# Four transposes per head instead of six, with the small probability blocks side by side

## The reference

```
# fox: forgetting attention
s = einsum(q, k) * scale + c[t] - c[s];  p = softmax(where(kpos <= qpos, s, NEG));  o = p @ v
# swa: window of 128, 2 kv heads, partial rotary, a sink per head in the denominator,
#      meta tokens (the first 16 keys) always visible
m = max(s_band.max, s_meta.max, sink);  denom = sum(p_band) + sum(p_meta) + exp(sink - m)
# mla: q and kv from low-rank latents, one rotary key shared by all heads
qf = [q_nope, rope(q_rope)];  kf = [k_nope, rope(k_rope)];  o = softmax(causal(qf @ kf)) @ v
# each: h = layer_norm(alpha * h + o @ w_o);  h = layer_norm(alpha * h + conv_glu_ffn(h))
```

## Time and profile before

| | |
|---|---|
| time, median of 3 runs | 1342.8 us (1342.38 to 1342.91) |
| profiled execution | 1340.74 us, of which span 1338.9 |
| PE busy | 1300.1 us, 97% of the span |
| DVE, ACT, POOL busy | 936.4, 816.1, 232.7 us |
| DMA | 202.81 MB, mean 151 GB/s |
| chain that ended last | PE 84%, DVE 7%, ACT 5%, issue 2% |
| in it | L381, L385, L384 23% each; L531 2%, L549 2% |

### The profile page before, as it was taken

The page is one execution under the profiler, slowest core; times in us unless marked ns, Lnnn a source line. Parts: engine busy times, 40 slices in busy tenths (PEclk is TensorE's granted clock), DMA queues, the critical chain, the costliest instruction groups (busy, mean ns, idle before and its releaser), DMA issues.

```text
span 1338.9 us, 30076 instructions
## 1 busy us (share of the span) xinstructions
PE 1300.1 (97%) x10437; PEld 1256.8 (94%) x10437; DVE 936.4 (70%) x1869; ACT 816.1 (61%) x1649; POOL 232.7 (17%) x216
## 2 busy tenths in 40 slices
PE   7999999999998999999998999999999999999997
PEld 7899999999987999999987899999999999999996
DVE  4865777765687877765678687776567666777764
ACT  5565766654565676664576677665456656766644
POOL 1000044420000034430001003433000000244300
PEclk9999999999999999999999999999999999999999
DMA  6432455556421455556442145555644333455572
GB/s 261 144 110 81 141 185 182 181 184 192 130 93 49 129 176 186 183 166 204 151 127 79 33 142 178 187 170 184 193 140 148 109 123 127 139 187 185 180 222 78
DMA packets 56724, 202.81 MB, mean 151 GB/s; under 512 B 6208, under 2 KB 8256, under 8 KB 56512
## 3 DMA queue, kind: packets, MB, share of 16 engines
q1 hardware_dynamic: 56640, 201.68, 46.8%
HBM read 200.61 MB, written 1.05 MB: 151 GB/s over the span
## 4 chain that ended last, share of the span: by engine, by line
PE 84%; DVE 7%; ACT 5%; issue 2%; DMA 1%; DVEq 0%; ACTq 0%; SPq 0%
PE ps L381 23%; PE ps L385 23%; PE ps L384 23%; PE ps L531 2%; PE ps L549 2%; DVE w_lo L1254 2%; PE ps L420 1%; ACT probs L885 1%; PE ps L514 1%; PE ps L426 1%; PE ps L423 1%; ACT w_hi L835 1%; DMA raw<-in_weights 1%; PE ps L495 1%; ACT L937 1%
## 5 line engine op out<-in xcount | busy, mean ns | idle before, releaser
L1254 DVE TENSOR_TENSOR w_lo<-raw,w_hi 128x1024 fp32r<-128x1024 f32 x377 | 460.9, 1224 | 228.5 <-ACT w_hi L835 226.8
L381 PE MATMUL ps<-h_hi,w_hi 128*128 128x272 f32 (+1 forms) x1752 | 509.3, 291 | 2.2 <-DVE q_rope L1511 1.0
L385 PE MATMUL ps<-h_hi,w_lo 128*128 128x272 f32 (+1 forms) x1752 | 503.4, 287 | 0.0
L384 PE MATMUL ps<-h_lo,w_hi 128*128 128x272 f32 (+1 forms) x1752 | 501.8, 286 | 0.0
L835 ACT ACTIVATE w_hi<-raw 128x1024 fp32r<-128x1024 f32 x377 | 395.3, 1050 | 151.0 <-PE ps L381 140.6
L381 PEld LDWEIGHTS ps<-h_hi,w_hi 128*128 128x128 f32 x1752 | 329.0, 188 | 9.0 <-issue 5.4
L384 PEld LDWEIGHTS ps<-h_lo,w_hi 128*128 128x128 f32 x1752 | 329.6, 188 | 0.3
L385 PEld LDWEIGHTS ps<-h_hi,w_lo 128*128 128x128 f32 x1752 | 329.1, 188 | 0.0
L381 PE MATMUL ps<-hid_hi,w_hi 128*128 128x272 f32 (+2 forms) x636 | 184.1, 289 | 0.3 <-ACT y L1087 0.2
L1228 POOL TENSOR_TENSOR gated<-y 128x272 f32<-128x272 f32 x88 | 134.6, 1530 | 276.3 <-DVE y L1666 261.7
L384 PE MATMUL ps<-hid_lo,w_hi 128*128 128x272 f32 (+2 forms) x636 | 182.0, 286 | 0.0
(11 more groups left out here) (187 smaller groups left out, 1757.3 us busy)
## 6 DMA issues: line engine op xcount, KB each, us to landing
raw<-in_weights SPq DMA_DIRECT2D x377, 512.0 KB, 3.7
cst<-in_consts SPq DMA_DIRECT2D x1, 1795.5 KB, 11.7
h<-in_x SPq DMA_DIRECT2D x2, 544.0 KB, 5.6
out<-h SPq DMA_DIRECT2D x8, 128.0 KB, 1.8
```

The source lines that it names most:

```text
L381: m = pe.matmul(b, whi, xhi, start=n == 0, stop=False)
L384: pe.matmul(b, whi, xlo, start=False, stop=False)
L385: m = pe.matmul(b, wlo, xhi, start=False, stop=n == len(tiles) - 1)
L1254: return dve.tensor_tensor(out_, a_, b_, op)
```

## The change

The score columns of a head are ordered anew. Chunk 1 comes first (0 to 143), then chunk 0 (144 to 159), then chunk 2 (160 to 431). The keys are stored with the last 16 tokens in front: `KCOL` says which columns a chunk takes, chunk 2 all of them and the others from column 16 on, so their 16 first keys come directly. In chunk 2 the last 16 keys stand first. `probs` has the same 432 columns per head as `scores`. Columns 128 to 175 of it now hold three blocks of 16 keys side by side: the end of chunk 1, all of chunk 0, and the last 16 keys of chunk 2. One transpose of 128 columns from 128 on turns them all, into partitions 0 to 47 (the rest of its rows is not used). Three more turn the large blocks. So:

- `turn`: four transposes of 128x128 per head.
- `copy_turned`: three copies, 128x384, 32x32 (two groups of 16 columns) and 16x16.
- `mix`: still three matmuls per head, of 272, 128 and 3 x 16 columns; the third is for the three small blocks and writes the first 16 columns of three stretches of 128.
- `v_tok`'s third block now needs on partitions 0 to 47 the values that go with them: a copy of the first 16 rows of its second block, of the first 16 rows of its first, and the last 16 tokens. ACT issues two small SBUF-to-SBUF DMAs per layer (`corner_values`), and the first mix of a layer waits for them.
- Each copy of keys is made in two parts, 16 and 256 columns; the rows of decays get one copy more; the masks' columns are rolled for chunk 2; fewer cells are cleared at the start.

```diff
-SCOL = (0, 16, 160, 432)
-PCOL = (0, P, 3 * P)
-PT1, PT2, PTW = T, T + P + TAIL, T + P + 2 * TAIL
+SCOL = ((P + TAIL, P + 2 * TAIL), (0, P + TAIL), (P + 2 * TAIL, P + 2 * TAIL + T))
+KCOL = ((TAIL, 2 * TAIL), (TAIL, P + 2 * TAIL), (0, T))
+TURNED = (0, P + 3 * TAIL, 2 * P + 3 * TAIL, P)
+PT1, PT2, PTW = T, T + P, T + P + 3 * TAIL
...
-        probs = sb("probs", [P, 4, PW])
+        probs = sb("probs", [P, 4, SW])
...
-                one(PT1 + TAIL - P, 1, P)
-                one(PTW - P, 2, 2 * P, TAIL)
-                one(0, 0, 0)
-                one(N_META, 1, 0)
-                one(N_META + P, 2, 0)
-                one(PT1 + TAIL, 2, P).then_inc(transposed, 1)
+                for n, col in enumerate(TURNED):
+                    t = pe.transpose(b[:, n * P:(n + 1) * P], pr[:, col:col + P], ident)
+                t.then_inc(transposed, 1)
...
+                if m == 0:
+                    pe.wait_ge(v_corners, 32 * (a + 1))
-                        ins = pe.matmul(ps[HD * s:HD * s + HD, 6, lo:T], v_tok[:, t, col:col + HD],
-                                        probs_t[:, s, c0:c0 + T - lo], start=n == 0, stop=n == 2)
+                        o, pt = ps[HD * s:HD * s + HD, 6], probs_t[:, s]
+                        if t < 2:
+                            dst, src = o[:, (0, N_META + P)[t]:T], pt[:, (0, PT1)[t]:(PT1, PT2)[t]]
+                        else:
+                            dst = o[:, 0:3 * P].rearrange("p (g c) -> p g c", g=3)[:, :, 0:TAIL]
+                            src = pt[:, PT2:PTW].rearrange("p (g c) -> p g c", g=3)
+                        ins = pe.matmul(dst, v_tok[:, t, col:col + HD], src, start=t == 0, stop=t == 2)
...
+            def corner_values(cols):
+                for n, chunk in enumerate((1, 0)):
+                    act.dma_start(v_tok[TAIL * n:TAIL * n + TAIL, 2, 0:cols],
+                                  v_tok[0:TAIL, chunk, 0:cols]).then_inc(v_corners, 16)
...
-                act.activation(probs_t[:, s, 0:PT2], ps[:, 4 + s, 0:PT2], ACT.Copy)
-                act.activation(probs_t[0:TAIL, s, PT2:PTW], ps[0:TAIL, 4 + s, PT2:PTW],
+                b = ps[:, 4 + s]
+                act.activation(probs_t[:, s, N_META:PT2], b[:, 0:3 * P], ACT.Copy)
+                act.activation(probs_t[0:32, s, PT2:PT2 + 2 * TAIL].rearrange("p (g c) -> p g c", g=2),
+                               b[0:32, 3 * P:4 * P].rearrange("p (g c) -> p g c", c=TAIL)[:, 0:8:7, :], ACT.Copy)
+                act.activation(probs_t[32:48, s, PT2 + 2 * TAIL:PTW], b[32:48, 4 * P - TAIL:4 * P],
                                ACT.Copy).then_inc(pt_copied, 1)
...
-                        copy(keys[:, m, :], b).then_inc(bank_free, 2)
+                        copy(keys[:, m, 0:TAIL], b[:, 2 * P:T])
+                        copy(keys[:, m, TAIL:T], b[:, 0:2 * P]).then_inc(bank_free, 2)
```

More of the change, by code:

```diff
@@ L228, in c @@
             return cst[0:rows, a:b]
+        rope_parts = scores[0:32].rearrange("p s c -> p (s c)")
         mean_sq, mean = y[:, 2, :], y[:, 3, :]
@@ L513, in score_pair @@
                         r = HD * s
-                        ins = pe.matmul(ps[0:hi_q - lo, 2 + s, SCOL[ch]:SCOL[ch + 1]],
-                                        queries[r:r + HD, m, lo:hi_q], keys[r:r + HD, m if fox else m // 4, 0:hi],
+                        ins = pe.matmul(ps[0:hi_q - lo, 2 + s, slice(*SCOL[ch])], queries[r:r + HD, m, lo:hi_q],
+                                        keys[r:r + HD, m if fox else m // 4, slice(*KCOL[ch])],
                                         start=not fox, stop=not fox or ch == 2)
@@ L544, in mix @@
                 pe.wait_ge(o_split, PAIRS * a + m)
-                for n, (t, lo, c0) in enumerate(((0, 0, 0), (1, P, PT1), (2, 2 * P, PT2))):
+                if m == 0:
+                    pe.wait_ge(v_corners, 32 * (a + 1))
+                for t in range(3):
                     for s in range(2):
@@ L1095, in copy_vt @@
                             act.wait_ge(lat_scale, 1)
-                        act.activation(v_tok[0:rows, chunk, half * 512:half * 512 + 512], ps[0:rows, 2 + n % 2],
+                        r0 = 32 if chunk == 2 else 0
+                        act.activation(v_tok[r0:r0 + rows, chunk, half * 512:half * 512 + 512], ps[0:rows, 2 + n % 2],
                                        ACT.Copy, scale=lat_col[0:rows, 1, chunk:chunk + 1]).then_inc(vt_copied, 1)
@@ L1527, in rope_keys @@
                             for r in range(2):
-                                ins = copy(keys[64 * r:64 * r + 64, g, :], q_rope[64 * g:64 * g + 64, 0, :])
+                                src = q_rope[64 * g:64 * g + 64, 0, :]
+                                copy(keys[64 * r:64 * r + 64, g, 0:TAIL], src[:, 2 * P:T])
+                                ins = copy(keys[64 * r:64 * r + 64, g, TAIL:T], src[:, 0:2 * P])
                         ins.then_inc(roped, 1)
@@ L1587, in rope_key_rows @@
                         dve.wait_ge(bank_free, LAYERS[a]["a"][2] + 6)
-                        own.link(tt(scores[0:32, 0, 0:T], gated[0:32, :], cos[0:32], ALU.mult))
+                        one, two, both = (rope_parts[:, n * T:n * T + T] for n in range(3))
+                        own.link(tt(one, gated[0:32, :], cos[0:32], ALU.mult))
                         dve.wait_ge(swapped, base)
-                        tt(scores[0:32, 1, 0:T], ps[0:32, 7, 0:T], sin[0:32], ALU.mult).then_inc(roped, 1)
+                        tt(two, ps[0:32, 7, 0:T], sin[0:32], ALU.mult).then_inc(roped, 1)
                         dve.wait_ge(roped, base)
-                        tt(scores[0:32, 0, 0:T], scores[0:32, 0, 0:T], scores[0:32, 1, 0:T],
-                           ALU.add).then_inc(key_roped, 1)
+                        tt(both[:, 0:TAIL], one[:, 2 * P:T], two[:, 2 * P:T], ALU.add)
+                        tt(both[:, TAIL:T], one[:, 0:2 * P], two[:, 0:2 * P], ALU.add).then_inc(key_roped, 1)
                     def rope_r(m):
@@ L1611, in take_k @@
                         b = bank(p, 2)
-                        tt(keys[0:64, 2 * m, :], b[0:64], kv_rstd[0:64], ALU.mult)
-                        tt(keys[0:64, 2 * m + 1, :], b[64:128], kv_rstd[64:128], ALU.mult).then_inc(bank_free, 2)
+                        for s in range(2):
+                            r = slice(HD * s, HD * s + HD)
+                            tt(keys[0:64, 2 * m + s, 0:TAIL], b[r, 2 * P:T], kv_rstd[r, 2 * P:T], ALU.mult)
+                            ins = tt(keys[0:64, 2 * m + s, TAIL:T], b[r, 0:2 * P], kv_rstd[r, 0:2 * P], ALU.mult)
+                        ins.then_inc(bank_free, 2)
                     gemm(a, "a", close_latent, links=None, straight=True)
@@ L1754, in masks @@
             seen = (k <= q) & ((q - k < window) | (k < N_META))
-            m[:hi - lo, SCOL[ch]:SCOL[ch + 1]] = np.where(seen, 0.0, NEG)
+            seen = np.roll(seen, TAIL, 1) if ch == 2 else seen
+            m[:hi - lo, slice(*SCOL[ch])] = np.where(seen, 0.0, NEG)
         both.append(m)
```

44 lines of the change are left out of this document (24 added, 20 removed).

## The result

The changed kernel takes 1352.5 us (median of 4, 1351.98 to 1355.43) against 1342.6 (1341.93 to 1342.91) for the kernel before: 9.9 us more, ratio 1.0082 with a 95% interval of 1.007 to 1.0095. The forecast was 1341.1, and its range ended at 1344.4.

What follows compares the result with a forecast made beforehand. PE bounds fox with the ACT/DVE loop 0.26 us behind; ACT and DVE pace SWA and MLA. Fox steady state -1.1, start +0.4, end -1.6, SWA +0.8, MLA -0.2 made -1.7: 1341.1 us, range 1339.0 to 1343.2 (whole 1336.9 to 1344.4).

Steps and rivals of the forecast that it cites:

- The bound: Fox steady state: PE sets the 9.80 us interval, the ACT and DVE loop has 0.26 us of slack behind it.
- the price of the added copy on ACT: ACT's added small copy of turned probabilities: +0.05 us per head, +0.10 per pair, bounds -0.02 to +0.13 per head.
- 12 x -0.09: Fox steady state: 0.09 us saved in each of six intervals in two layers, -1.1 us.
- SWA's seven intervals: SWA: turned copies lie in ACT's half of the loop, +0.10 us in each of seven intervals, +0.7.
- The DMA issues: Two small DMAs per layer issued by ACT: nothing in fox (0.92 us wait) and SWA, +0.1 in MLA, bounds 0 to 0.9.
- rival D's sign: MLA: ACT gap of 0.5 us or more at the DMAs; issue +0.9 or longer half-clock stretch, 1342 to 1344, chance 0.07.
- Rival C: ACT between transposes and w_hi: each added small copy costs its whole duration, +0.13 per head; 1345.6 us, chance 0.15.
- Rival B's milder sum: Whole kernel: small operations free, second loop holds, 0.26 saved per fox interval; -5.9 us, 1336.9; chance of B 0.25.
- the time of the transposes at fox's ends: Fox end: last two pairs turned where PE is the bound, -0.82 us per layer, -1.6 in all.
- the small keys copies: DVE: keys copied in two parts, small copies spaced 0.08 us, +0.07 each, bounds 0 and +0.17.
- the stride of the mixes: PE: third mix writes with a stride, between 0 and another 0.05 us, taken as 0; PE's fox loop 9.42.
- MLA was forecast at -0.2: MLA: keys and latent's key rows +0.3, DMA issues +0.1, end keys and copies +0.2, last transposes two pairs x -0.41.

Runs made afterwards that it cites:

- the copy at partition 0: Kernel before plus one more small ACT copy per head, 16 partitions from partition 0, into an unread place: 1341.9 us, ratio 0.9995.
- the copy at partition 32: Kernel before plus one more small ACT copy per head, 16 partitions from partition 32, into an unread place: 1352.0 us against 1342.3, ratio 1.0063.

## Why the prediction was wrong

- **The bound was right.** In fox the loop through scores, masks, exps, copies, w_hi, w_lo and keys stood 0.26 behind PE: with the transposes taken away it shows at 9.54, and with the copies as I priced them at 9.70 (forecast 9.71).
- **The step that failed** is the price of the added copy on ACT: "the added one costs about 0.08, so +0.05 per head and +0.10 per pair", with the bounds -0.02 and +0.13. It is +0.29 per head, over twice the upper bound. I took the spacing of a copy on partition 0 between others on partition 0; the third copy is on partitions 32 to 47, and neither it nor the one behind it overlaps with the one ahead, so that two overlaps are lost. My upper bound charged the one instruction as long as it lasts, and nothing to its neighbours. That turned 12 x -0.09 into 12 x +0.41 (+6.0 against the forecast) and SWA's seven intervals from +0.7 into +3.5 (+2.8). Together 8.8 of the 11.6 us by which the change in time (+9.9) missed the forecast one (-1.7).
- The trace before had rows that pointed to it. DVE's four keys copies, whose source and output change between partitions 0 and 64, take 1.23 for four, 0.31 apart, and one lasts 0.29 to 0.30: no overlap. And of ACT's copies of MLA's queries, whose source changes from partitions 0 to 63 to partitions 64 to 127, the second starts 0.40 behind the first, which lasts 0.39:

```profile
708.50 0.18 ACT L885 ACTIVATION_READ_ACCUMULATOR probs<-scores,stats 128x1 f32 x1
708.71 0.80 ACT L1104 ACTIVATE queries<-ps 64x272 f32<-64x272 f32 x2
709.41 0.29 ACT L885 ACTIVATE probs<-scores,stats 16x16 f32<-16x16 f32 x1
```

- **The DMA issues** in fox, taken at nothing for 0.92 of idle time: they occupy 1.27, and cost 0.42 in the first layer and 0.75 in the second, where only 0.50 of idle time stood (L885 at 1036.44 above); I took the first layer's row for both. That is 1.2 us more of the 11.6. The 0.59 per issue of SP was in hand; I used it for MLA only. There, rival D's sign, a gap on ACT of 0.5 or more, did not come: the issues run beside a w_hi, and the gap is 0.22.

```profile
708.62 1.18 ACTq L876 DMA_DIRECT2D v_tok<-v_tok  x2
709.89 1.06 ACT L834 ACTIVATE w_hi<-raw 128x1024 fp32r<-128x1024 f32 x1 [0.22 <-issue]
```

- Rival C had the right place and the right sign. Its price, a duration in full, would have given 1345.6; and its ground, that short instructions cost their length, is refuted by the copy at partition 0.
- Rival B's milder sum, -5.9, is what the transposes are worth alone (1335.3 against 1341.2). That the small operations are free, its condition, was wrong for the copy at partition 32 and nearly right for the one at 0. Right were also the time of the transposes at fox's ends (0.44 saved per pair, -0.88 per layer against -0.82), the small keys copies (0.08) and the stride of the mixes (9.38 on PE against 9.42).
- MLA was forecast at -0.2. The traces of the changed kernel lie between +0.7 and +3.0 and those of the kernel before between 0 and +1.5. At equal clock the change itself costs some 0.5 there by the table above, an estimate from a few traces. Whether it also makes the falls longer stays open: 13.7 us at the lower level is seen in four traces, all of kernels with the new order of columns, and in none of the eight with the old one. The rest of the 11.6 us, 1.6, probably lies there and in the fall in SWA; no experiment here settles it.

## What to carry to other kernels

Price a small instruction in a packed stretch by rows with the same change of partitions before and behind it, not by its size alone; one that reads and writes at other partitions than its neighbours costs itself and both overlaps (0.31 us here, against 0.06). When work is taken from the bounding engine, find the loop just behind it, and write first what that loop waits for: here the order of w_hi and the copies was worth some 9 us in the changed kernel (1352.5 to 1342.9, or by the ratios to the kernel before 1.0082 to 1.0017), and nothing in the one before. An issue of a DMA is work on the queue that issues it, of 0.6 us here; look for its idle time in every layer in which it stands.

## What the runs showed of the hardware

- ACT lets the next instruction start 0.09 us before the end of the one ahead when both begin at the same partition, also with 128 partitions ahead of 16 and with a strided source. Where the begin differs, the next starts 0.01 to 0.03 behind the end. Only the begins 0, 32 and 64 occur here. It is enough that one side, source or output, differs. The last 16 tokens' values, read at partition 0 and written to 32, are 0.28 ahead of the next copy in the changed kernel, and 0.17 when written to 0; both last 0.27:

```profile
46.99 0.27 ACT L869 ACTIVATE v_tok<-ps 16x128 f32<-16x128 f32 x1
47.27 0.38 ACT L870 ACTIVATE v_tok<-ps 128x256 f32<-128x256 f32 x1
```

```profile
46.02 0.27 ACT L870 ACTIVATE v_tok<-ps 16x128 f32<-16x128 f32 x1 [2.00 <-PE ps L485]
46.19 0.36 ACT L871 ACTIVATE v_tok<-ps 128x256 f32<-128x256 f32 x1
```

- What is compared is not always the instruction just ahead. In the rows of MLA's queries above, the exps that read SBUF start at 709.41, 0.10 before the copy from partition 64 of PSUM ends. The next copy that reads PSUM from partition 0 has no overlap, as the one at 708.71 shows, 0.02 behind an instruction that begins at 0 like itself. And in the changed kernel out_hi doesn't overlap with the w_hi ahead of it, although both begin at 0, when the last one that read PSUM was the copy at 32:

```profile
406.29 1.04 ACT L834 ACTIVATE w_hi<-raw 128x1024 fp32r<-128x1024 f32 x1
407.35 0.40 ACT L912 ACTIVATE hid_hi<-ps 128x272 fp32r<-128x272 f32 x1
```

- All rows of ACT agree with this reading: an instruction can overlap only if its source begins where the last one that read the same memory (PSUM or SBUF) did, and its output where the last output did. Counted with the partitions that the kernel's lines name, 202 of ACT's instructions in the trace of the changed kernel differ in that, and none of them overlaps with the one ahead; of the other 1484, which may also wait for other engines, 1041 do. In the kernel before only 16 differ. The 186 more, at 0.09 of lost overlap each, make some 17 of the 20.2 us by which ACT's busy time grew (an estimate). Why it is so, no run here shows.

- The granted clock falls to the lower level in MLA, where PE idles most, and not alike in executions of one kernel: 3.4 or 10.2 us in all in the kernel before, 6.8 or 13.7 in the changed one. In the changed kernel that moves the stage by up to 2.3 us.
